# The mLSTM value projection moved ahead of the attention, as seven-product slabs, in a hybrid decoder layer

## The reference, cut to what matters

```python
(q, k_c, v_c, k_s, v_s, k_w, v_w, g_nsa, mq, mk, mv, mo, mi, mf, cu) = jnp.split(h @ w_in, points, axis=-1)
a_out = nsa_attention(q, k_c, v_c, k_s, v_s, k_w, v_w, g_nsa, ...)      # 16 heads, 4 key groups
a_out = head_rmsnorm(a_out, NSA_HEADS, nsa_out_g)
hm = mlstm_chunkwise(mq, mk, mv, mi + mlstm_i_bias, mf + mlstm_f_bias)    # 4 heads; needs mv
hm = head_rmsnorm(sigmoid(mo) * hm, MLSTM_HEADS, mlstm_out_g)             # mo is the output gate
c = silu(layernorm(causal_depthwise_conv(ca * sigmoid(cg), conv_w, conv_b), ...))
x = x + jnp.concatenate([a_out, hm, c], axis=-1) @ w_out
x = x + hier_moe(rmsnorm(x), ...)                                         # 32 experts of 2048 x 512 x 3
```

## Time and profile before

| | us |
|---|---|
| median of 3 runs (lowest, highest) | 1419.67 (1419.46, 1420.44) |
| the profiled execution, its own time | 1420.33 |
| its span | 1418.5 |
| PE busy (share) | 1214.9 (86%) |
| DVE busy | 490.5 (35%) |
| ACT busy | 253.4 (18%) |

### The profile page before, as it was taken

How to read it: one execution, slowest core, us unless ns; L and a number is a source line. 1 busy time by engine, 2 the same in 40 slices (tenths; PEclk the granted TensorE clock), 3 DMA queues, 4 the chain that set the end, 5 groups by cost and what they waited for, 6 DMA issues and landing times.

```text
span 1418.5 us, 18090 instructions
## 1 busy us (share of the span) xinstructions
PE 1214.9 (86%) x7509; PEld 710.0 (50%) x7509; DVE 490.5 (35%) x1016; ACT 253.4 (18%) x628; POOL 18.8 (1%) x88
## 2 busy tenths in 40 slices
PE   8999999999999998768699958768697696877976
PEld 6999999766568753233244314224242241422422
DVE  5599997663876431121010310111101111011113
ACT  3001111444600222011111102002020020200212
POOL 2000000000010000000000000000000000000001
PEclk9999999999999999789899978889889898887999
DMA  9958577431644899999999999999999999999996
GB/s 300 323 179 168 152 157 238 119 80 41 179 116 166 361 419 428 427 428 428 426 428 427 427 427 428 428 427 428 428 427 429 427 428 428 426 428 428 427 428 261
DMA packets 133539, 479.35 MB, mean 338 GB/s; under 512 B 47980, under 2 KB 105808, under 8 KB 107728
## 3 DMA queue, kind: packets, MB, share of 16 engines
q1 hardware_dynamic: 126816, 477.58, 86.4%
q10 hardware_dynamic: 6640, 0.58, 0.4%
HBM read 476.05 MB, written 2.10 MB: 337 GB/s over the span
## 4 chain that ended last, share of the span: by engine, by line
PE 54%; DMA 42%; DVE 2%; ACT 1%; issue 1%; POOLq 0%; POOL 0%; SPq 0%; ACTq 0%; DVEq 0%
DMA ring<-in_expert_w_up_dram 33%; PE PS L1146 14%; PE PS L1487 10%; DMA spare<-in_expert_w_up_dram 6%; PE PS L1295 5%; PE PS L1474 4%; PE PS L1188 3%; PE PS L1272 2%; PE PS L1677 2%; DMA ring<-in_expert_w_down_dram 2%; PE PS L1465 1%; PE PS L1549 1%; PE PS L965 1%; PE PS L1687 1%; PE PS L1138 1%; PE PS L1207 1%
## 5 line engine op out<-in xcount | busy, mean ns | idle before, releaser
L1487 PE MATMUL PS<-ring,XG 128*32 128x512 f32 x1296 | 233.3, 767 | 133.0 <-DMA ring<-in_expert_w_up_dram 94.4
L1487 PEld LDWEIGHTS PS<-ring,XG 128*32 128x32 f32 x1296 | 58.2, 136 | 266.5 <-issue 263.3
L3156 DVE TENSOR_TENSOR hTe<-PS,sg 128x128 f32<-128x128 f32 (+1 forms) x31 | 9.9, 319 | 339.8 <-ACT sg L2266 339.6
L2972 DVE TENSOR_TENSOR x<-PS,x 128x1024 f32<-128x1024 f32 x41 | 50.2, 1224 | 218.0 <-PE PS L1566 216.1
L1474 PE MATMUL PS<-ring,XG 128*64 128x512 f32 x192 | 93.1, 642 | 17.7 <-DMA ring<-in_expert_w_up_dram 15.0
L2253 ACT ACTIVATE Hs<-PS 128x512 f32<-128x512 f32 x30 | 17.9, 597 | 464.6 <-PE PS L1487 343.4
L1476 PE MATMUL PS<-ring,XG 128*64 128x512 f32 x192 | 91.7, 634 | 0.0
L1566 PE MATMUL PS<-Y,SW 128*128 128x512 f32 (+2 forms) x176 | 89.0, 616 | 1.5 <-ACT ro L2362 1.5
L1487 PE MATMUL PS<-spare,XG 128*32 128x512 f32 x208 | 68.6, 820 | 23.3 <-DMA ring<-in_expert_w_up_dram 23.1
L1465 PEld LDWEIGHTS PS<-sel,xn 128*128 128x128 f32 x640 | 75.3, 191 | 12.9 <-issue 12.7
L1146 PE MATMUL PS<-hT,ring 128*128 128x128 f32 x672 | 78.8, 275 | 0.0
(11 more groups left out here) (508 smaller groups left out, 1568.2 us busy)
## 6 DMA issues: line engine op xcount, KB each, us to landing
ring<-in_expert_w_up_dram SPq DMA_DIRECT2D x53, 2048.0 KB, 23.0
ring<-in_expert_w_gate_dram SPq DMA_DIRECT2D x53, 2048.0 KB, 26.8
ring<-in_expert_w_down_dram SPq DMA_DIRECT2D x51, 2048.0 KB, 26.5
ring<-in_w_in_dram SPq DMA_DIRECT2D x17, 2048.0 KB, 11.4
spare<-in_expert_w_gate_dram SPq DMA_DIRECT2D x9, 2048.0 KB, 25.9
spare<-in_expert_w_up_dram SPq DMA_DIRECT2D x8, 2048.0 KB, 22.9
spare<-in_expert_w_down_dram SPq DMA_DIRECT2D x8, 2048.0 KB, 27.0
ring<-in_w_in_dram SPq DMA_DIRECT2D x16, 512.0 KB, 6.8
```

The lines of the kernel that those rows point to most:

```text
L1487: mm = pe.matmul(PS[r:r + 32, 0, :], gathered_rows(q, 4 * c + j)[:, column:column + 32], weight_rows(slots[u], 4 * (c % 2) + j), start=(c ...
L2972: dve.tensor_tensor(y, new, old, ALU.add).then_inc(sc_added, 1)
```

## The change

The slabs `mv0` and `mv1` join `FAST_SLABS`: they are multiplied with seven products each, right after `vw0` and before the attention. `LATE` now begins at `mo`, and the plain steps are 64. For these two slabs DVE's temporaries are other tiles, as `mv` and `mo` are about to be filled: two parts of `att` (the tile `spare`), and `mo`. The list of PE's work is written anew: the same attention, with fewer plain steps between its parts; the convolution's part of `out_part` 0 and 1 stands in `scores(3)`, in four quarters; the first four head features of `out_part(0)` stand between `attend(2)` and `attend(3)`.

```diff
-FAST_SLABS = (..., "q3", "vw0")
+FAST_SLABS = (..., "q3", "vw0", "mv0", "mv1")
-LATE = units_before("mv")
+LATE = units_before("mo")
-        in_t3, in_t2 = (... for tile in (mv, mo))
+        mv_k, mo_k = (... for tile in (mv, mo))
+        att_low, att_high = (att[:, c:c + 1024].rearrange("p (k n) -> p k n", k=8) for c in (0, 3072))
+        MV = len(FAST) - 2
+        def in_t3(j):
+            return {MV: att_high, MV + 1: mo_k}.get(j, mv_k)
+        def in_t2(j):
+            return att_low if j >= MV else mo_k
...
-            def scores(s, steps):
+            def scores(s, steps, between=None):
...
                         fill(steps)
+                        if between is not None:
+                            between(i)
...
+            def conv_quarter(i):
+                out_part(i // 2, conv_f[2 * (i % 2):2 * (i % 2) + 2], i % 2 == 0, False)
-            fill(8)
+            fill(4)
             pe.wait_ge(unit_saved, LATE)
             pe.wait_ge(cmp_saved, 3)
             scores(0, 2)
-            scores(1, 3)
-            fill(16)
+            scores(1, 2)
+            fill(12)
             pe.wait_ge(sT_ready, ML_H)
-            attend(0, 4)
-            scores(2, 3)
-            attend(1, 4)
+            attend(0, 0)
+            scores(2, 4)
+            attend(1, 0)
             mean_square(0)
-            scores(3, 3)
-            fill(LATE_STEPS)
-            mlstm_values()
             pe.wait_ge(conv_out, CT)
             pe.wait_ge(unit_saved, len(UNITS))
-            out_part(0, conv_f, True, False)
+            scores(3, 0, conv_quarter)
+            mlstm_values()
             mean_square(1)
             attend(2, 0)
-            out_part(1, conv_f, True, False)
+            out_part(0, head_f[0:4], False, False)
             attend(3, 0)
             mlstm_columns()
             mean_square(2)
             pe.wait_ge(hm_out, ML_H)
-            out_part(0, ml_f + head_f, False, True)
+            out_part(0, ml_f + head_f[4:8], False, True)
             mean_square(3)
             out_part(1, ml_f + head_f, False, True)
...
-            exponents(1, 1)
+            exponents(1, 0)
...
-            attend_saves(0, 1)
+            attend_saves(0, 0)
...
-            attend_saves(1, 1)
+            attend_saves(1, 0)
...
-            late_saves(1)
...
-            finish(15)
+            follow(15)
+            follow(16)
+            finish(17)
```

More of the change, by code:

```diff
@@ L191 @@
 UNITS = projection_units()
-FAST_SLABS = ("cg1", "ca0", "ca1", "mq0", "mq1", "mk0", "mk1", "vc0", "ks0", "kw0", "vs0", "q0", "q1", "q2", "q3", "vw0")
+FAST_SLABS = ("cg1", "ca0", "ca1", "mq0", "mq1", "mk0", "mk1", "vc0", "ks0", "kw0", "vs0", "q0", "q1", "q2", "q3", "vw0", "mv0",
+              "mv1")
 FAST = [u for u, (n, _, kind, _, i) in enumerate(UNITS) if SLABS[n] in FAST_SLABS and i == 0]
@@ L433, in build @@
         tok_21, tok_22 = hT[:, 0:8, P:2 * P], hT[:, 8:16, P:2 * P]
-        in_t3, in_t2 = (tile[:, :, :].rearrange("p a b -> p (a b)").rearrange("p (k n) -> p k n", k=8) for tile in (mv, mo))
+        mv_k, mo_k = (tile[:, :, :].rearrange("p a b -> p (a b)").rearrange("p (k n) -> p k n", k=8) for tile in (mv, mo))
+        att_low, att_high = (att[:, c:c + 1024].rearrange("p (k n) -> p k n", k=8) for c in (0, 3072))
[4 more added lines that the diff above has]
+            return att_low if j >= MV else mo_k
         def quarter(u, high, right):
@@ L1161, in fast_products @@
                 fast_product(u, "m5", tok_s1, quarter(u, 0, 1)).then_inc(prod_done, 1)
-                fast_product(u, "m7", tok_s3, in_t3)
+                fast_product(u, "m7", tok_s3, in_t3(j))
                 pe.wait_ge(w_summed, 4 * j + 3)
-                fast_product(u, "m6", tok_s2, in_t2)
+                fast_product(u, "m6", tok_s2, in_t2(j))
                 pe.wait_ge(w_summed, 4 * j + 4)
@@ L2460, in left_sums @@
                     dve.wait_ge(unit_done, FAST[j - 1] + 2)
-                dve.tensor_tensor(in_t3, quarter(u, 1, 1), quarter(u, 0, 1), ALU.subtract)\
+                dve.tensor_tensor(in_t3(j), quarter(u, 1, 1), quarter(u, 0, 1), ALU.subtract)\
                     .then_inc(w_summed, 1)
@@ L2468, in right_sum @@
                 dve.wait_ge(w_summed, 4 * j + 2)
-                dve.tensor_tensor(in_t2, quarter(u, 1, 1), quarter(u, 0, 1), ALU.subtract)\
+                dve.tensor_tensor(in_t2(j), quarter(u, 1, 1), quarter(u, 0, 1), ALU.subtract)\
                     .then_inc(w_summed, 1)
@@ L2475, in last_sum @@
                 dve.wait_ge(w_summed, 4 * j + 3)
-                dve.tensor_tensor(quarter(u, 1, 0), quarter(u, 1, 0), in_t2, ALU.subtract)\
+                dve.tensor_tensor(quarter(u, 1, 0), quarter(u, 1, 0), in_t2(j), ALU.subtract)\
                     .then_inc(w_summed, 1)
```

## The result

The changed kernel took 1430.66 us (median of 4 runs, 1428.75 to 1432.0); the kernel before took 1419.57 us in the same series (4 runs, 1419.41 to 1420.44). The ratio is 1.0076 [1.0064, 1.0088]: slower by 0.76%, 11 us. The forecast of 1427.0 had the sign and two thirds of the size, and the result lies in its range. In the profiled execution (1430.67 us, span 1428.7) the span grew by 10.2 us.

A forecast was written before the change was run, and what follows sets the result against it. Expert-weight DMA fills two thirds of the run but starts when PE gets there; before it, chains between engines decide. The terms put the seven-product block 7.3 us later, 414.8 against 407.46, giving 1427.0 us, range 1422 to 1432.

The forecast's parts named there:

- Two slabs ahead, scores(0) and scores(1): Start of the attention: the slabs' products take 25.02 us, scores(0) begins 23.8 later, attend(0) regains 2.0 at DVE's pace.
- Attend without steps, scores(2) with four: attend(0) takes 9.3 us, 8.9 sooner; ACT then sets attend(1)'s second transposes at 350.7, PE waiting about 1.8.
- mean_square(1): After scores(3): DVE's chain of 8.26 us comes last, PE waits 3.1 us, and mean_square(1) comes at 375.9.
- The tail: Last head features of v = 1 wait for head_norm(3) on DVE until 411.3; the 3.5 us taken out give 0.6.
- The clock: Rival for PE's new waits between 291 and 415: each clock drop costs up to 2.2 us, 1429 to 1431.5; chance 0.13.
- The sum: Chain to the first seven-product block: 414.8 against 407.46 us, 7.3 us later, so 1427.0 us.
- the forecast as worked out: Main case, the chain of waits up to the first seven-product block: 1425.3 to 1429.5 us, chance 0.60.
- PE's share of 98%: Rival for the stage from 264 to 407 us: PE alone bounds it, 2.6 to 3.4 us less, 1416.7; chance 0.07.
- The expert stream: Rival for the expert loads: their start is not set by PE, the delay is swallowed, time stays at 1420; chance 0.10.
- The terms in brackets behind the sum: Parts up to the seven-product block: +23.8, -2.0, -8.9, +1.8, -8.0, +1.6, -0.5, -0.6, giving 7.3 us later.
- The bounds of the parts: Low and high values for single parts of the chain; together they were said to give a shift of 5.8 to 10 us.

The follow-up runs named there:

- the reordering of DVE: The changed kernel with head_norm(3) moved ahead of the three weight sums on DVE; 1425.19 us, 1.0043 of the kernel before.
- the fitted list: The changed kernel with mv1's units in banks 6 and 7, steps and convolution features dealt into waits, head_norm(3) ahead of weight sums; 1418.07 us, 0.9995 of the kernel before.

## Why the prediction was right, and what it left out

The chain of the forecast against the profiled execution (us):

```
                                     forecast   measured
scores(0)                              291.3     291.2
attend(0), behind DVE's line           328.5     328.2
scores(2)                              337.8     337.8
second transposes of attend(1)         350.7     350.8
scores(3)                              360.0     360.1
mean_square(1), behind DVE             375.9     376.0
first mLSTM features                   393.8     395.4
last four head features, behind DVE    411.3     412.9
first seven-product block              414.8     418.1
```

*Two slabs ahead, scores(0) and scores(1).* Right: 25.0 us for the products, 0.54 us of wait against 0.6, biases at DVE's pace, and a wait of 2.19 against 2.4.

*Attend without steps, scores(2) with four.* Right within 0.3 us, with ACT last before the second transposes (1.66 against 1.8). That the new temporaries and the shifted slab loads cost nothing is borne out: the products of the two slabs follow one another for 25.0 us without a wait.

*mean_square(1).* Right: the block that had hidden DVE's chain is ahead of it, and PE waits 2.91 us (forecast 3.1). From the last pair of scores(3) to mean_square(1) it is 8.23 us (367.81 to 376.04), before 8.26, so DVE did not run slower.

*The tail.* Right in its cause and size, 2.67 us against 2.6; the reordering of DVE removed just that wait.

*The clock.* This is what was missed, as a choice rather than as a mechanism. The sum has nothing for it, and its rival had a chance of 0.13, for the reason that "Nothing here shows a wait of 3 us alone". That step failed. From mean_square(1) to the first mLSTM features it is 19.33 us where the sum had 17.9, and the last eight out instructions take 5.24 to the next block where it had 3.5. That is 1.4 and 1.7 us, 3.1 of the 3.3 by which the block is late. The measured 1430.66 lies in the rival's 1429 to 1431.5 for one or two drops, and above the 1425.3 to 1429.5 of the forecast as worked out. Its price of up to 2.2 us a drop is an upper bound that holds: the falls measured here cost 1.2 to 2.2 us. The Trainium skill, TensorE: Matmul & The Clock Gate, section "HAM oscillation — how this bites in real kernels", has it that a matmul kernel whose pauses are long enough is slowed again behind every one of them. By that rule the change costs more than its waits, and the trace agrees for two of the four waits here, with 1.4 and 1.7 us.

*The rivals that fell.* PE's share of 98% was no bound: with 2.8 us of PE work less (25.0 for 27.8), and the rest in a new order, the kernel is 11 us slower. The expert stream swallowed nearly nothing: 10.7 us at the seven-product block, and still 10.7 at the expert load shown above, are 10.2 at the end.

*Slips in the working.* The slices have nine tenths from the fifteenth on (496 us), not the fourteenth, which has eight; nothing rests on it. The terms in brackets behind the sum do not all fit their parts: by the times that the parts give, scores(2) adds 1.3 and not 1.8, attend(1) takes off 7.5 and not 8.0, scores(3) adds 1.2 and not 1.6, and the stretch to the head features nothing; the total is the same 7.3. The bounds of the parts taken together reach 11.5 and not 10. So the shift of 10.7 us lies inside what the parts allowed, though the parts that had room (the slabs, attend(0), attend(1)) came out within 0.3 us of the values that were taken and the clock took the room instead.

What stays open is the 0.5 us between 10.7 and 10.2, lost behind 512 us, and which of the four waits has a fall behind it in a given run.

## What to carry to other kernels

An engine that is busy 98% of a stage may be so because fillers stand in the waits of a chain between other engines; before its work is made cheaper or moved, work out the chain without the fillers and see which wait each of them covers. If new waits of 2 us or more appear on TensorE, or several of 1 us in a row, count a fall of the clock behind them as a likely term of the sum and not as a remote rival (here 1.2 to 2.2 us each, behind some and not behind others); matmuls whose result nobody reads, sized to the wait, show how much of a loss is clock and how much is waiting. And when a list of one engine's work is reordered, the order in which the others free its buffers has to move with it.

## What the runs showed of the hardware

- A wait of the same length at the same place of the same program (2.91 and 2.92 us) was followed by a lower clock in one execution (0.60) and not in another (1.00). The wait of 2.2 us before attend(0) had a fall behind it in two kernels (16 transposes in 3.28 and 3.47 us) and none in the two profiled runs of the change. Three waits of only 1.0 to 1.1 us in a row had a fall behind them (0.50 in the window). The wait of 1.66 us before the second transposes of attend(1) had none (1.00) in both runs of the change and in the five variants that keep it (one of them with 1.67). So in these runs the length of one wait does not tell whether the clock falls. The Trainium skill, TensorE: Matmul & The Clock Gate, section "What's actually happening", says of the start of a kernel that the number of matmuls at the lower clock differs between runs of the same kernel. No run here looks at the start; behind a wait it differed likewise, by the 0.60 and 1.00 above.
- The clock also fell with no wait of PE over a third of a microsecond in the eight before: with the fitted list the router's ten products took 5.81 us in two executions (0.65 and 0.72 in the window from 490 to 494 us) and 4.11 in a third (1.00), with one wait of 0.31 us ahead of them in all three. They also took 5.81 us in the profiled runs of the kernels with the last head norm first and with the convolution in blocks. What made it fall there is open.
- A float32 matmul of 128x128x128 is two instructions in the trace and took 0.223 us at a clock of 1.00 (26 in 5.8 us); sized by one instruction, a filler comes out twice too long.
